# Two layers and a mixture of experts on one core: how the next layer's shift and scale are formed in the first layer

## The reference, cut to what matters

```python
c_act = jax.nn.silu(c)
for l in range(DEPTH):                                   # DEPTH = 2
    mod = c_act @ w_ada[l] + b_ada[l]                    # 1024 -> 3 * 1024
    shift, scale, gate = split_cols(mod, (D, D, D))
    h = rms_norm(x, g_pre[l]) * (1.0 + scale) + shift
    ... = split_cols(h @ w_in[l], IN_SPLITS)
    ...                                                  # three attention branches, each gated
    y = (g[:, :, 0] * o_a + g[:, :, 1] * o_b + g[:, :, 2] * o_c) @ w_out[l]
    x = x + gate * rms_norm(y, g_post[l])
```

## Time and profile before

| | us |
|---|---|
| median of 3 runs | 2291.82 |
| lowest and highest run | 2291.10, 2293.22 |
| the profiled execution | 2289.33 |
| its span, from the first instruction to the last | 2287.5 |
| PE busy in the span | 1786.9 (78%) |
| DVE busy | 506.2 (22%) |
| ACT busy | 312.8 (14%) |
| POOL busy | 53.8 (2%) |
| mean DMA rate | 312 GB/s |

### The profile page before, as it was taken

One profiled execution on the slowest core, in us unless ns is written; L12 is line 12 of the kernel. 1 busy time (PEld: TensorE's weight loads), 2 busy tenths in 40 slices (PEclk: granted clock), 3 DMA queues, 4 the chain that ended last, 5 costly groups with the idle time before them and its releaser, 6 DMA issues.

```text
span 2287.5 us, 23801 instructions
## 1 busy us (share of the span) xinstructions
PE 1786.9 (78%) x10294; PEld 1012.6 (44%) x10294; DVE 506.2 (22%) x1137; ACT 312.8 (14%) x740; POOL 53.8 (2%) x93
## 2 busy tenths in 40 slices
PE   7999999999999999998656666566665656666666
PEld 4877785877785677553212222121222212222212
DVE  3254322154322354642000000000100000000001
ACT  1123401123411022320000000000000000000001
POOL 1000000000003000100000000000000000000000
PEclk9999999999999999999778778777877878887777
DMA  9674453454463424389999999999999999999996
GB/s 330 200 237 174 163 169 105 169 191 173 170 214 128 149 93 148 124 330 399 427 429 426 427 428 428 427 427 430 426 428 428 427 428 425 429 428 428 427 428 275
DMA packets 126367, 714.31 MB, mean 312 GB/s; under 512 B 11561, under 2 KB 16233, under 8 KB 96447
## 3 DMA queue, kind: packets, MB, share of 16 engines
q1 hardware_dynamic: 117840, 698.12, 75.2%
q10 hardware_dynamic: 6151, 8.77, 1.2%
q0 software_dynamic: 2272, 5.90, 1.1%
HBM read 708.95 MB, written 3.80 MB: 312 GB/s over the span
## 4 chain that ended last, share of the span: by engine, by line
PE 50%; DMA 45%; DVE 2%; SPq 1%; ACT 1%; issue 1%; POOL 0%; DVEq 0%; ACTq 0%; POOLq 0%
DMA arena<-in_w_up_dram 22%; DMA arena<-in_w_down_dram 21%; PE banks L871 14%; PE banks L2707 5%; PE banks L1857 4%; PE banks L937 4%; PE banks L1862 3%; PE banks L945 2%; PE banks L2739 2%; PE banks L2747 2%; DMA arena<-in_w_mods_dram 2%; PE banks L1001 1%; PE banks L1029 1%; PE banks L1011 1%; PE banks L957 1%
## 5 line engine op out<-in xcount | busy, mean ns | idle before, releaser
L2707 PE MATMUL banks<-arena 128*32 128x512 f32 (+2 forms) x3072 | 421.6, 687 | 327.0 <-DMA arena<-in_w_up_dram 327.0
L2707 PEld LDWEIGHTS banks<-arena 128*32 128x32 f32 x3072 | 132.2, 132 | 585.7 <-issue 582.5
L871 PE MATMUL banks<-arena 128*128 128x256 f32 x1536 | 343.0, 380 | 0.0
L871 PEld LDWEIGHTS banks<-arena 128*128 128x128 f32 x1536 | 288.1, 190 | 40.5 <-issue 3.7
L2739 PE MATMUL banks<-arena 128*32 128x512 f32 x1280 | 206.0, 795 | 91.8 <-DMA arena<-in_w_down_dram 91.8
L2739 PEld LDWEIGHTS banks<-arena 128*32 128x32 f32 x1280 | 44.5, 133 | 227.6 <-DMA arena<-in_w_down_dram 127.4
L2835 DVE SCALAR_TENSOR_TENSOR arena<-arena,banks 64x512 f32<-64x512 f32 (+1 forms) x48 | 30.5, 634 | 516.4 <-ACT arena L2758 515.4
L2758 ACT ACTIVATE arena<-banks 64x512 f32<-64x512 f32 (+1 forms) x48 | 26.6, 554 | 819.9 <-PE banks L2707 818.5
L1857 PE MATMUL banks<-arena 128*128 128x256 f32 x512 | 113.6, 380 | 1.4 <-DVE arena L2271 0.7
L1857 PEld LDWEIGHTS banks<-arena 128*128 128x128 f32 x512 | 96.1, 190 | 16.1 <-issue 3.8
L2842 DVE COPY arena<-banks 128x512 f32<-128x512 f32 x16 | 11.1, 691 | 347.5 <-PE banks L2748 347.5
(11 more groups left out here) (346 smaller groups left out, 1655.2 us busy)
## 6 DMA issues: line engine op xcount, KB each, us to landing
arena<-in_w_gate_dram SPq DMA_DIRECT2D x60, 2752.0 KB, 35.9
arena<-in_w_up_dram SPq DMA_DIRECT2D x60, 2752.0 KB, 32.7
arena<-in_w_down_dram SPq DMA_DIRECT2D x64, 2048.0 KB, 31.3
arena<-in_w_in_dram SPq DMA_DIRECT2D x68, 1024.0 KB, 8.3
arena<-in_w_mods_dram SPq DMA_DIRECT2D x48, 1024.0 KB, 7.4
arena<-in_w_down_dram SPq DMA_DIRECT2D x32, 1024.0 KB, 27.1
arena<-in_w_out_dram SPq DMA_DIRECT2D x12, 1024.0 KB, 5.1
arena<-in_w_gate_dram SPq DMA_DIRECT2D x8, 1376.0 KB, 11.4
```

What stands on the lines that cost most here:

```text
L871: mm = pe.matmul(b[:, i * S:i * S + S], w, rhs[:, kt, :], start=kt == 0, stop=kt == 7)
L2707: mm = pe.matmul(bank[pc][32 * g:32 * g + 32, 0:w_], xsT[:, kt, CAP * e4:CAP * e4 + CAP], (wg if g < 2 else wu)[:, c:c + w_], start=kt == ...
```

## The change

In layer 0 alone, the four `ada` and the four `modT` jobs are computed in another way. POOL weighs the loads itself: for each of the two loads of a quarter it multiplies the four blocks with their condition values (one number for each partition and block, repeated along 512 columns, in place in the ring slot), adds the two halves of the result (1024 numbers for each partition), and those again (512). At the end it adds the sums of both loads. What stands in `mrow` is then a sum over eight of the 1024 input rows for each partition. PE adds over the partitions: each block of 128 columns is the stationary operand of a product with a single column of ones, so that the result is a column. Job `ada` n makes the first two columns of quarter n, `modT` n the other two. ACT copies the first two to `mcv`, DVE the others. The gates of layer 0, layer 1 and the third block stay as they were.

PE's job `ada` n waits for POOL's last addition (`next_sum`), and POOL waits for the ring slots (`ring_full`), for its own instruction before, and from quarter 2 on for `modT` n-2, whose `mrow` half it writes again. The ring slots of the weights are given back by the same jobs as before.

```diff
@@ PE, in job()
-                    if kind == "ada":
+                    if l == 0 and kind in ("ada", "modT"):
+                        first = 0 if kind == "ada" else 2
+                        if kind == "ada":
+                            pe.wait_ge(next_sum.sem, next_sum.at(0, n + 1))
+                        else:
+                            pe.wait_ge(reader(l, JOB_OF["ada", n]), taken(l, JOB_OF["ada", n]))
+                        for i in range(2):
+                            c = 512 * (n % 2) + (first + i) * P
+                            mm = pe.matmul(b[:, i:i + 1], mrow[:, c:c + P], ones[:, 0:1], start=True, stop=True)
+                    elif kind == "ada":
@@ ACT, in the fill jobs
+                        elif kind == "ada" and l == 0:
+                            nc.scalar.copy(mcv[:, 4 * n:4 * n + 2, 0], bank_of(l, j)[:, 0:2]).then_inc(reader(l, j), 1)
@@ POOL, in the layer loop, behind the transfers of the bias
+                if l == 0:
+                    for n in range(4):
+                        acc = mrow[:, 512 * (n % 2):512 * (n % 2) + 512]
+                        if n >= 2:
+                            pool.wait_ge(job_done.sem, made(0, JOB_OF["modT", n - 2]))
+                        for half, i in enumerate(JOBS[JOB_OF["ada", n]][2]):
+                            s_ = turn_of(0, i) % RING
+                            pool.wait_ge(ring_full[s_], 16 * (turn_of(0, i) // RING + 1))
+                            w = view(ring[:, s_, :], 4, 512)
+                            nc.gpsimd.tensor_tensor(w, w, cav[:, 4 * half:4 * half + 4, 0:1].to_broadcast([P, 4, 512]),
+                                                    ALU.mult).then_inc(next_own.sem, next_own.up())
+                            pool.wait_ge(next_own.sem, next_own.last())
+                            nc.gpsimd.tensor_tensor(w[:, 0:2, :], w[:, 0:2, :], w[:, 2:4, :], ALU.add).then_inc(next_own.sem, next_own.up())
+                            pool.wait_ge(next_own.sem, next_own.last())
+                            outp = w[:, 0, :] if half else acc
+                            nc.gpsimd.tensor_tensor(outp, w[:, 0, :], w[:, 1, :], ALU.add).then_inc(next_own.sem, next_own.up())
+                            pool.wait_ge(next_own.sem, next_own.last())
+                        nc.gpsimd.tensor_tensor(acc, acc, w[:, 0, :], ALU.add).then_inc(next_sum.sem, next_sum.up())
@@ DVE, columns(n)
+                    if l == 0:
+                        nc.vector.tensor_copy(mcv[:, 4 * n + 2:4 * n + 4, 0], bank_of(l, j)[:, 0:2]).then_inc(reader(l, j), 1)
+                        return
```

More of the change, by code:

```diff
@@ L640, in blocks_kernel @@
         cols1 = Signal(sem("modulation_columns_1"))
+        next_own, next_sum = Signal(pro_a.sem, base=1), Signal(pro_c.sem, base=3)
         gate_read, gate_sum = Signal(sem("gate_weights_read"), 2), Signal(sem("gate_summed"), 2)
```

## The result

The changed kernel takes 2312.03 us in the median (2309.61 to 2312.3, four runs), the kernel before 2291.63 in the runs beside it. The ratio is 1.0089, with a 95% interval of 1.0077 to 1.0101: slower by 20 us. The forecast was 2306, with 2285 to 2325 as its range. The profiled execution's span is 2310.1 us, 22.6 more than before.

A forecast was written before the change was run, and what follows sets the result against it. PE was taken to bound the changed stretch. Waits of 21.7 us less 5.9 saved gave +15.8 on 2289.33, so 2305.1 profiled and 2307.6 from the median; the prediction was 2306, range 2285 to 2325.

The forecast's parts named there:

- The forecast's term: In layer 0's stretch, DVE's two-input or SBUF-to-SBUF instructions and POOL's take whole-instruction turns; +7 to +36 us, chance 0.58.
- my walk: Instruction-by-instruction reckoning of DVE held by POOL; in quarter 1, unit 11, it made PE wait 9.2 us.
- 216.8 - 205.8: Unit 11, quarter 1: probabilities ready on DVE at 216.8 us instead of 205.8.
- The waits for DVE: PE's waits before transposes in quarters 0 to 3: 5, 9.2, 4.5 and 3 us, 21.7 in all.
- The last sentence of the prediction: A granted clock below 1.00 behind PE's new waits would be a cost not counted; no size given.
- the sum of +15.8: Net change of the whole program: 21.7 us of waits less 5.9 us spared on PE.
- PE's saving: In the `ada` and `modT` jobs, 10.3 us become 4.2; the gain of 6.1 us was taken as 5.9.
- Both run beside PE, and I price them at nothing: ACT's smaller copy and DVE's small copy in place of its reduction cost PE nothing.
- POOL late at the `ada` jobs: POOL's sums late by some 2.5 us in each of three quarters, contained in PE's waits for DVE.
- the second case of the rivals: Engines undisturbed, but PE waits for late sums at `ada` jobs: +1.6 to +12 us, 2291; chance 0.12.
- case 1: Engines undisturbed, POOL quick, sums in time up to 2.0 ns an element: 5.9 us faster, median 2286; chance 0.17.
- Case 3: DVE and POOL take turns, but POOL's instructions are short (0.84 ns an element): -1 us, 2288 to 2290; chance 0.13.

The follow-up runs named there:

- the kernel with GpSimd beside: Kernel before the change, plus GpSimd doing the sums' seven instructions per quarter on a buffer nobody reads: 2311.56 us, ratio 1.0088.
- the VectorE version: Changed kernel with the weighted sums on VectorE instead of GpSimd, eight instructions of 512 columns per quarter: 2287.92 us, ratio 0.9987 to the kernel before.
- the first experiment: Changed kernel without GpSimd's sums; PE waits for the two loads and multiplies what stands in the buffer: 2286.31 us, ratio 0.9979 to the kernel before.

## Why the prediction was right

**The direction and the mechanism.** The forecast's term, that a DVE instruction waits for POOL's running one, was its open one and is what the runs show. Its details are not all as forecast. In unit 11 the maximum's last step (L1527, now L1560) escaped, half a microsecond ahead of POOL's product. The reciprocal behind it ran beside the product in its usual 0.17 us, and L1576, the former L1543, was held in its place. Then the L1548 and the L1554 did not go in as pairs between two instructions of POOL, as in my walk: each of the four waited for one of its own. The unit's end was put back by 11.0 us (12.75 - 1.73), just the 216.8 - 205.8 of the forecast, and that the two agree so well is luck: one hold fewer at the start, two more behind, and a shorter product. With GpSimd on quarter 1 alone, and in the kernel with GpSimd beside, the start of the walk did happen (3.43 and 3.50 us for the 0.17 of the maximum's last step). POOL hardly waits for DVE in return, 0.34 us at most. PE's wait at unit 11 was 7.8 us against 9.2.

**The sizes.** The waits for DVE were put at 5, 9.2, 4.5 and 3 us for the four quarters, 21.7 in all. Measured: 3.19, 7.82, 2.70 and 0.15, so 13.9. This is the term that was mis-sized, by 7.8 us. Two things can make the difference: POOL's product, 3.64 us instead of 4.5; and the units stood otherwise against POOL's instructions, since each delay of PE also puts off the next quarter's loads. How much each of the two makes was not measured apart.

**What was not in the sum: the clock.** The last sentence of the prediction named a granted clock below 1.00 behind the new waits as a cost not counted. By the lengths of the products behind the waits it was 8.5 us, and filling three of the waits gave 5 to 7 back. So the sum of +15.8 is near the measured +20 in part by luck: 7.8 us too much for the held instructions, 8.5 missing for the clock, and 3.2 missing for the short waits and for POOL's last sum (below).

**PE's saving.** 5.9 us was right as work (3.9 to 4.4 us for the new products against 4.2), confirmed by the VectorE version's 3.8 plus 2.25, which is 6.1. "Both run beside PE, and I price them at nothing" was right for the copies, but an earlier PE met waits for ACT and DVE, 0.70, 0.23 and 0.90, so 1.8 us of the 5.9. They stand in the first experiment too, where GpSimd does nothing.

**POOL late at the `ada` jobs.** I said that the waits for DVE would contain it. They did for quarters 0 to 2. In quarter 3, where DVE delays PE least, PE waited 1.37 us for L1368. That is the second case of the rivals, and its share grows as the contention shrinks (1.29 and 3.21 us with short pieces). The limit given for case 1, sums in time up to 2.0 ns for an element, doesn't follow from the forecast's own numbers: at 2.0 ns a quarter takes 17.1 us with the handovers, and 22.1 us behind the issue is later than the 20.2 to 20.7 between the jobs. The limit is 1.8 ns.

**The first and third case.** Without the sums the gain is there, 5 us. That was about the right price for case 1. Case 3, turns with short instructions, is near to what cutting the pieces made, +12 us, much more than my -1. My case had GpSimd's total at 31 us (7.7 a quarter) and no cost of clock; with the pieces the total is 70 us, and the lower clock alone costs about 7.

## What to carry to other kernels

An idle GpSimd is not free capacity where VectorE is on the path: look at which VectorE instructions fall into its instructions, by their operands (here those from SBUF to SBUF, but not reductions, reciprocals or forms with an input in PSUM), and at how many follow each other, since each can be held for a whole one. If the work must go there, cut it short or lay it beside units with slack; here VectorE itself, with eight blocks placed in its own waits, did the same work 24 us better. Where PE is the bound, count a new wait at its length plus what the granted clock costs behind it. That was half as much again in the changed kernel, a third with GpSimd beside and with quarter 1 alone, 0.8 of the waits with short pieces, and nothing in the VectorE version.

## What the runs showed of the hardware that I had not expected

- Cutting GpSimd's instructions to 512 columns made its work 9% longer (69.9 us against 64.4) and still took 9 us off the time.
- A product with a repeated second operand is cheaper on GpSimd than an addition with two full ones: 1.09 us for 512 elements against 1.28 in the short pieces. Whether the operand or the operation makes it was not tried apart.
- Two numbers for each partition are enough to be held: L1576 of 128x2 took 2.64 us. A reciprocal of the same 128x2 (L1569) is not: 0.17 us beside GpSimd's product.
- In the experiment with the columns alone the clock fell to 0.73 around 222 to 226 us, behind waits of 0.23 and 0.90 us only. With waits of 0.59 and 0.90 at the same place it stayed at full speed in the VectorE version's execution, and so it did behind 0.23 and 0.90 in the changed kernel (24 records in 5.34 us from 238.74 on). What decides between them stays open; the time is 1.7 us.
